# First vectors in eight blocks, turns between two units, attention heads in pairs, a norm's second weights behind its root, and a gate unit three tiles ahead

## The chip, the cores and the metric

The kernel runs on one NeuronCore of a Trainium2 chip. The metric is the time of one execution on the device, in microseconds (us). Five engines work side by side, each through its own instruction list in order, and wait for one another on semaphores: TensorE (PE, matmuls), VectorE (DVE), ScalarE (ACT), GpSimd (POOL) and SyncE (SP). Here POOL and SP only start DMAs. PEld is TensorE's weight load, which overlaps its matmuls. TensorE's clock has two levels, 1.2 and 2.4 GHz, which the profile shows as 0.5 and 1.0.

## The reference

Two layers over 256 latent tokens and 256 context tokens, width 1024, all in float32.

```python
for l in range(DEPTH):                                  # DEPTH = 2
    ml = ada_params(c, mod_w[l], mod_b[l])              # silu(c) @ (1024 x 9216): 9 vectors of 1024
    mc = ada_params(c_ctx, mod_w[l], mod_b[l])
    xl = ffn_half(xl, ml[0:3], ...); xc = ffn_half(xc, mc[0:3], ...)
    hl = modulate(rmsnorm(xl, mix_norm[l]), ml[3], ml[4]); ...
    # even layer: conv group (GLU, depthwise conv 31, LayerNorm, swish) + windowed attention,
    #             8 heads of 64, 2 key heads; odd layer: bidirectional chunked mLSTM
    xl = xl + ml[5] * yl
    xl = ffn_half(xl, ml[6:9], ...); ...
return rmsnorm(xl, final_norm)

def ffn_half(x, mods, g, w_gu, w_d):
    shift, scale, gate = mods
    h = modulate(rmsnorm(x, g), shift, scale) @ w_gu    # 1024 x 5632
    hg, hu = jnp.split(h, 2, axis=-1)
    return x + 0.5 * gate * ((jax.nn.silu(hg) * hu) @ w_d)
```

## The kernel before

Activations lie features on partitions, tokens along the row (512: latent, then context), in 8 tiles of 128 features. Each big product is made of three reduced-precision matmuls (`three`, L429 to L434): high by high, high by low, low by high. The order of every engine is written out by hand.

- **Units.** Weights come in units of 1 MB (`load`, SP). ScalarE copies a unit's high part (`head`, L877), VectorE subtracts to get its low part (`rest`, L1176), TensorE multiplies (`unit`, L444). `raw`, `w_hi`, `w_lo` and two PSUM banks per unit are double: a unit's matmuls start when its low part is made and the unit two before it has been read out (`begin`, L439). A unit is 48 matmuls of 512 columns: 8 tiles, 2 halves, 3 each.
- **Norm n** (0 to 6). ScalarE squares the 8 tiles (L916, L963), VectorE adds them (L1189), TensorE sums over features (L487), ScalarE takes the root (L887), VectorE makes a diagonal of reciprocals (L1214, L1215), TensorE spreads it (L492), and then tile by tile VectorE scales (L1237, `t_ring`), ScalarE rounds to the high part (L895, `hn_hi`), VectorE makes the low part (L1253, `hn_lo`). The first unit behind a norm takes each tile as it comes; the second starts when the first is through.
- **Vectors.** The 18 modulation vectors are 18 jobs. A job is 4 MB of `mod_w` in 4 quarters (`mod_raw`), 16 matmuls for two conditions in each (`mod_products`, L468, four column groups of 32), a copy by ScalarE (`mod_rows`, L910), two small matmuls that turn it (`mod_columns`, L477), and the bias by VectorE (`mod_vector`, L1265). Jobs 0 and 1 stand ahead of the first FFN; others lie behind units, in norms, and jobs 6 to 11 in the attention, a quarter per turn from turn 10 on. A quarter's DMA is started by GpSimd when the quarter before it in its place has been used.
- **Attention** (turns j = 0 to 31, one per head and 128 queries; `s` 0 latent with 512 keys, 1 context with 256). TensorE: `scores` L606, `turn` L615 (transposes), `values` L632. VectorE: `largest` L1402 or L1405, `denominator` L1414, `hn_lo` L1426. ScalarE: `expo` L998, `normalise` L1006, `turned` L1013, `att_head` L1019. Between them VectorE does the depthwise convolution (`taps`, L1359, 124 of 512 elements, 28 of them ahead of turn 0) and TensorE the last two convolution units (`conv_step`), whose sigmoids (L1033) ScalarE does in turns 4 and 9 with a table load before and behind. LayerNorm (L662) follows when all taps are done.
- **od_gate.** Behind norm 4 TensorE does the gate unit (16 columns) and the first key unit tile by tile together (from L703 on), then turns the gate rows (L720); VectorE reads them (L1486), which frees the bank for the next unit.

## Time and profile before

| | us |
|---|---|
| median of 3 runs | 1926.68 (1919.63, 1926.95, 1926.68) |
| profiled execution | 1918.44 |
| its span, first to last instruction | 1916.7 |
| TensorE busy | 1819.4 (95%) |
| VectorE busy | 869.5 (45%) |
| ScalarE busy | 626.4 (33%) |
| mean granted clock of TensorE | 0.974 |

The chain that ended last is TensorE for 90% of the span. The engines' rows give busy time; what matters for this change are the few stretches where TensorE is not full: the start, the norms, the attention and the gate unit.

### The profile page before, as it was taken

The numbers are of one execution on the slowest core, as the hardware profiler recorded it, in microseconds if no ns is written. First come the engines' busy times: TensorE is split into PE (matmuls) and PEld (weight loads), VectorE is DVE, ScalarE is ACT, GpSimd is POOL, SyncE is SP. The second block draws the span as 40 slices with busy tenths as digits, with TensorE's granted clock in tenths as the row PEclk, the third lists the DMA queues.
The fourth block names the chain that finished last, engine by engine and source line by source line (L and its number), as shares of the span: only waits on it lengthen the run. The fifth ranks groups of instructions, "written<-read, shape, count | busy, mean of one in ns | idle before, by whom it ended". The sixth has DMA issues, their size and how long they took to land.

```text
span 1916.7 us, 25184 instructions
## 1 busy us (share of the span) xinstructions
PE 1819.4 (95%) x10083; PEld 1490.1 (78%) x10083; DVE 869.5 (45%) x1335; ACT 626.4 (33%) x849; POOL 36.2 (2%) x72
## 2 busy tenths in 40 slices
PE   3999999999889999999999999999998999899996
PEld 1788888877544668888888688888886998889996
DVE  2433332345878663333233633333344436765554
ACT  2332122223445432222222432222224323544342
POOL 0000000000001000000000000000000000000000
PEclk7999999999899989999999999999998999999998
DMA  8522452243138444222323422233123212354543
GB/s 340 225 88 88 176 191 94 69 153 146 45 130 309 154 158 172 103 83 101 109 71 101 180 88 95 86 105 109 63 93 153 88 67 90 110 197 174 188 170 105
DMA packets 39107, 252.39 MB, mean 132 GB/s; under 512 B 4464, under 2 KB 5872, under 8 KB 14448
## 3 DMA queue, kind: packets, MB, share of 16 engines
q1 hardware_dynamic: 29232, 179.91, 26.5%
q0 software_dynamic: 9792, 71.31, 9.7%
q8 instruction: 61, 1.00, 0.2%
q14 instruction: 22, 0.18, 0.0%
HBM read 250.15 MB, written 1.05 MB: 131 GB/s over the span
## 4 chain that ended last, share of the span: by engine, by line
PE 90%; DVE 5%; ACT 2%; issue 1%; DMA 1%; SPq 0%; ACTq 0%; DVEq 0%
PE ps L432 27%; PE ps L434 27%; PE ps L433 27%; PE ps L468 3%; DVE w_lo L1176 1%; PE ps L632 1%; DMA xT<-in_xT 1%; DVE y L1359 1%; PE ps L606 1%; PE ps L745 1%; PE ps L774 1%; PE ps L492 1%; ACT w_hi L877 1%; PE ps L615 1%; DVE acc L1189 0%
## 5 line engine op out<-in xcount | busy, mean ns | idle before, releaser
L432 PE MATMUL ps<-hn_hi,w_hi 128*128 128x512 f32 (+2 forms) x1784 | 648.6, 364 | 10.2 <-DVE hn_lo L1253 8.3
L433 PE MATMUL ps<-hn_lo,w_hi 128*128 128x512 f32 (+2 forms) x1784 | 640.8, 359 | 0.0
L434 PE MATMUL ps<-hn_hi,w_lo 128*128 128x512 f32 (+2 forms) x1784 | 640.4, 359 | 0.0
L1176 DVE TENSOR_TENSOR w_lo<-raw,w_hi 128x2048 fp32r<-128x2048 f32 (+2 forms) x184 | 377.0, 2049 | 566.3 <-ACT w_hi L877 566.1
L877 ACT ACTIVATE w_hi<-raw 128x2048 fp32r<-128x2048 f32 (+2 forms) x184 | 316.6, 1721 | 777.5 <-PE ps L434 774.1
L432 PEld LDWEIGHTS ps<-hn_hi,w_hi 128*128 128x128 f32 (+1 forms) x1784 | 339.5, 190 | 74.8 <-issue 21.8
L434 PEld LDWEIGHTS ps<-hn_hi,w_lo 128*128 128x128 f32 (+1 forms) x1784 | 339.4, 190 | 50.5
L433 PEld LDWEIGHTS ps<-hn_lo,w_hi 128*128 128x128 f32 (+1 forms) x1784 | 339.8, 190 | 48.6 <-issue 0.5
L432 PE MATMUL ps<-a_hi,w_hi 128*128 128x512 f32 (+1 forms) x704 | 255.6, 363 | 1.7 <-DVE a_lo L1291 1.7
L433 PE MATMUL ps<-a_lo,w_hi 128*128 128x512 f32 (+1 forms) x704 | 255.2, 363 | 0.0
L434 PE MATMUL ps<-a_hi,w_lo 128*128 128x512 f32 (+1 forms) x704 | 255.2, 362 | 0.0
L1194 DVE SCALAR_TENSOR_TENSOR xT<-ps,modT,xT 128x256 f32 (+1 forms) x136 | 59.9, 480 | 226.0 <-PE ps L434 226.0
L432 PEld LDWEIGHTS ps<-a_hi,w_hi 128*128 128x128 f32 x704 | 132.9, 189 | 23.0 <-DVE a_lo L1291 2.1
L434 PEld LDWEIGHTS ps<-a_hi,w_lo 128*128 128x128 f32 x704 | 132.9, 189 | 20.7
L433 PEld LDWEIGHTS ps<-a_lo,w_hi 128*128 128x128 f32 x704 | 132.9, 189 | 20.5
L935 ACT ACTIVATE a_hi<-prod 128x512 f32 (+3 forms) x88 | 50.9, 579 | 212.4 <-DVE prod L1288 212.4
L468 PE MATMUL ps<-mod_raw,c_act 128*32 128x256 f32 x1152 | 81.4, 417 | 17.3 <-DMA mod_raw<-in_mod_w 13.6
L1291 DVE TENSOR_TENSOR a_lo<-prod,a_hi 128x512 f32 (+3 forms) x88 | 55.1, 626 | 71.8 <-ACT a_hi L935 71.8
L1359 DVE SCALAR_TENSOR_TENSOR y<-upad,cols,y 128x512 f32<-128x512 f32 x120 | 82.0, 744 | 0.0
L468 PEld LDWEIGHTS ps<-mod_raw,c_act 128*32 128x32 f32 x1152 | 34.2, 117 | 60.5 <-issue 34.4
L432 PE MATMUL ps<-w_hi,hn_hi 128*128 128x256 f32 x256 | 77.1, 301 | 4.1 <-DVE shared L1486 4.1
L433 PE MATMUL ps<-w_lo,hn_hi 128*128 128x256 f32 x256 | 73.4, 287 | 0.0
(189 smaller groups left out, 1162.4 us busy)
## 6 DMA issues: line engine op xcount, KB each, us to landing
raw<-in_w_up SPq DMA_DIRECT2D x88, 1024.0 KB, 4.8
mod_raw<-in_mod_w POOLq DMA_DIRECT2D x68, 1024.0 KB, 7.3
raw<-in_w_downA SPq DMA_DIRECT2D x32, 768.0 KB, 4.3
raw<-in_w_downB SPq DMA_DIRECT2D x32, 640.0 KB, 3.9
raw<-in_w_od_in SPq DMA_DIRECT2D x16, 1024.0 KB, 4.8
raw<-in_w_ev_in SPq DMA_DIRECT2D x7, 1024.0 KB, 4.8
mod_raw<-in_mod_w SPq DMA_DIRECT2D x4, 1024.0 KB, 10.1
raw<-in_w_ev_out SPq DMA_DIRECT2D x4, 1024.0 KB, 4.8
```

Of the source, the lines that this page charges most:

```text
L432: pe.matmul(o, lh, rh, start=first, stop=False)
L433: pe.matmul(o, lh, rl, start=False, stop=False)
L434: return pe.matmul(o, ll, rh, start=False, stop=last)
L468: last = pe.matmul(ps[32 * g:32 * g + 32, product_bank(m), 0:LAT], c_act[:, k, :], mod_raw[:, k, g * LAT:(g + 1) * LAT], start=(k == 0), s ...
L492: pe.matmul(ps[:, 7, 0:W[n]], ones, rstd[:, 0:W[n]], start=True, stop=True).then_inc(rstd_mm, 1)
L606: pe.matmul(ps[:, 4 + j % 2, k0:KEYS], qk[64 * h2:64 * h2 + 64, tt, a:a + P], qk[64 * h2:64 * h2 + 64, CT, k0:KEYS], start=True, stop=True ...
L877: act.activation(w_hi[:, u0 % 2, 0:n], raw[:, u0 % 2, 0:n], ACT.Copy).then_inc(hi_made, 1)
L935: act.activation(a_hi[:, j + 2 * r, 0:w], prod[:, j, 0:w], ACT.Copy).then_inc(a_hi_made, 1)
L1176: dve.tensor_tensor(w_lo[:, u0 % 2, 0:n], raw[:, u0 % 2, 0:n], w_hi[:, u0 % 2, 0:n], ALU.subtract).then_inc(lo_made, 1)
L1194: last = dve.scalar_tensor_tensor(out=xT[:, d0 + 2 * r, tokens(s)], in0=ps[:, bank(u0, b), tokens(s)], scalar=modT[:, vec, d0 + 2 * r, s:s ...
L1291: dve.tensor_tensor(a_lo[:, j + 2 * r, 0:w], prod[:, j, 0:w], a_hi[:, j + 2 * r, 0:w], ALU.subtract).then_inc(a_made, 1)
L1359: ins = dve.scalar_tensor_tensor(out=dst, in0=src, scalar=col("conv_w", i * CT + c), in1=dst, op0=ALU.mult, op1=ALU.add)
```

## The change

- **First vectors.** Jobs 0 and 1 (shift and scale of norm 0) are laid out anew in 8 blocks of 1 MB: block b holds what tile b of both vectors needs. SP loads `x` first (in 4 parts), then the blocks, two first weight units among them. TensorE does norm 0 ahead of all blocks. The vectors of tile k + 1 are then made while tile k is multiplied: `block_columns(k + 1)` stands behind tile k's matmuls of the first unit, `block_products` behind later ones. GpSimd starts with job 2.
- **Two units in turns.** Behind norms 0, 1, 2, 3 and 5 the first two units share the tiles as they come: 5 tiles in turns (2 for 256 tokens), then the rest of the first unit, then the rest of the second. A job that lay between them still does.
- **Norms.** The first square goes straight into `acc`, the last is added by TensorE (8 small matmuls in place of 4), the clear of `acc` goes. The second unit's high and low part (`LATE_UNIT`) move from ahead of the norm to behind the root.
- **Attention.** 16 turns of a pair of heads in place of 32; `values` alternates the two heads' column groups; context scores share one bank with a wait (`s_half`) and other work between; two quarters of a job per turn; 30 early taps; sigmoids in turns 3 and 9; one pair of banks for the transposes and one for the values in place of two.
- **Gate unit.** It runs alone for three tiles; the keys follow three tiles behind; its rows are turned inside the key unit.

```diff
@@ sync
-            for q in range(4):
-                sp.dma_start(mod_raw[:, 2 * q:2 * q + 2], t["mod_w"][0][:, 2 * q:2 * q + 2]).then_inc(mod_first[q], 16)
-            sp.dma_start(xT[:], t["xT"]).then_inc(x_in, 16)
+            for i in range(4):
+                sp.dma_start(xT[:, 2 * i:2 * i + 2], t["xT"][:, 2 * i:2 * i + 2]).then_inc(x_in[i], 16)
...
+            block(0)
             load(U["f0upA"], 0, 0, t["w_up"][0, 0], UNIT)
+            block(1)
+            load(U["f0upA"], 1, 0, t["w_up"][0, 1], UNIT)
+            for b in range(2, KT):
+                block(b)
@@ tensor
+            def first_units(u0, n, w, between=None):
+                ready = hn_ready(n)
+                order = [(j, k) for k in range(side(w)) for j in range(2)]
+                order += [(j, k) for j in range(2) for k in range(side(w), KT)]
+                for j, k in order:
...
+                    if k == KT - 1:
+                        last.then_inc(unit_mm, 1)
+                        if j == 0 and between:
+                            between()
+                    if n == 0 and j == 0 and k + 1 < KT:
+                        block_columns(k + 1)
+                    if n == 0 and (j, k) in PRODUCTS_BEHIND:
+                        block_products(PRODUCTS_BEHIND[j, k])
...
             def turn(j):
-                if j >= 2:
-                    pe.wait_ge(pT_made, j - 1)
+                if j >= 1:
+                    pe.wait_ge(pT_made, j)
...
+            def values(tt, s):
+                g = 2 * tt + s
+                pe.wait_ge(pT_made, 4 * tt + 2 + s + 1)
+                if g >= 1:
+                    pe.wait_ge(mix_made, g)
...
+                for i, kt in enumerate(att_keys(s)):
+                    for h2 in range(2):
+                        last = pe.matmul(ps[64 * h2:64 * h2 + 64, 0, 0:LAT], v_att[:, kt, 64 * h2:64 * h2 + 64],
+                                         turned_place(s)[:, h2, i, :], start=(i == 0), stop=(kt == 3))
...
+            BEHIND = 3
+            for step in range(KT + BEHIND):
+                if step < KT:
...
+                    last = three(ps[0:16, bank(u), :], weights(u, k * 16, (k + 1) * 16), ...)
+                if step >= BEHIND:
+                    k = step - BEHIND
...
+                    if k < 4:
+                        mod_products(KEY_JOB, k, k + 1)
...
+                    if k == 6:
+                        pe.wait_ge(gate_rows, 1)
@@ scalar
             def norm(n):
                 norm_root(n)
+                head_of(LATE_UNIT[n])
...
+            for k in range(KT):
+                if k == 1:
+                    head_of(1)
+                norm_head(0, k)
+                if k + 1 < KT:
+                    block_rows(k + 1)
@@ vector
             def norm(n):
                 norm_gain(n)
                 norm_rstd(n)
+                rest_of(LATE_UNIT[n])
                 norm_apply(n)
...
+            for k in range(KT):
+                block_vectors(k)
+                norm_scaled(0, k)
+                norm_rest(0, k)
+                if k == 0:
+                    rest_of(1)
```

TensorE ahead of and in the first FFN's first unit, before. `mod_raw` is a job's data, `shared` its row; L432 to L434 are one product in three.

```order
L468 MATMUL ps<-mod_raw,c_act 32x256 [waits mod_in3]
L468 MATMUL ps<-mod_raw,c_act 32x256 x7
L477 MATMUL ps<-sel,shared 128x8 [waits mod_made,mod_row]
L477 MATMUL ps<-sel,shared 128x8
L432 MATMUL ps<-hn_hi,w_hi 128x512 [waits hn_made,lo_made]
L433 MATMUL ps<-hn_lo,w_hi 128x512
L434 MATMUL ps<-hn_hi,w_lo 128x512
L432 MATMUL ps<-hn_hi,w_hi 128x512
```

And after, from the second tile of the first unit on.

```order
L477 MATMUL ps<-hn_hi,w_hi 128x512 [waits hn_made]
L478 MATMUL ps<-hn_lo,w_hi 128x512
L479 MATMUL ps<-hn_hi,w_lo 128x512
L477 MATMUL ps<-hn_hi,w_hi 128x512
L478 MATMUL ps<-hn_lo,w_hi 128x512
L479 MATMUL ps<-hn_hi,w_lo 128x512
L538 MATMUL ps<-sel,shared 128x2 [waits mod_made,mod_row]
L538 MATMUL ps<-sel,shared 128x2
L477 MATMUL ps<-hn_hi,w_hi 128x512
L478 MATMUL ps<-hn_lo,w_hi 128x512
```

The small matmuls that turn the vector of the next tile (`ps<-sel,shared`) stand between the two units' matmuls of a tile, and wait for a row.

VectorE at the end of the first FFN and in the norm behind it, before (`acc` the sum of squares, `w_lo` the low part of weights).

```order
L1194 SCALAR_TENSOR_TENSOR xT<-ps,modT,xT 128x256 [waits unit_mm]
L1194 SCALAR_TENSOR_TENSOR xT<-ps,modT,xT 128x256
L1189 TENSOR_TENSOR acc<-acc,sq 128x512 [waits sq_added,sq_made]
L1176 TENSOR_TENSOR w_lo<-raw,w_hi 128x2048 [waits hi_made]
L1206 SCALAR_TENSOR_TENSOR modT<-modT,cols 128x8 [waits mod_made]
L1206 SCALAR_TENSOR_TENSOR modT<-modT,cols 128x8
L1214 RECIPROCAL inv<-inv 128x4 [waits sd_made,link_v]
L1215 TENSOR_TENSOR rstd<-mats,inv 128x512 [waits link_v]
L1219 MEMSET acc 128x512
L1237 SCALAR_TENSOR_TENSOR t_ring<-xT,modT,ps 128x256 [waits rstd_mm,acc_clear]
```

And after.

```order
L1322 SCALAR_TENSOR_TENSOR xT<-ps,modT,xT 128x256 [waits unit_mm]
L1322 SCALAR_TENSOR_TENSOR xT<-ps,modT,xT 128x256
L1334 SCALAR_TENSOR_TENSOR modT<-modT,cols 128x8 [waits mod_made]
L1334 SCALAR_TENSOR_TENSOR modT<-modT,cols 128x8
L1342 RECIPROCAL inv<-inv 128x4 [waits sd_made,link_v]
L1343 TENSOR_TENSOR rstd<-mats,inv 128x512 [waits link_v]
L1303 TENSOR_TENSOR w_lo<-raw,w_hi 128x2048 [waits hi_made]
L1359 SCALAR_TENSOR_TENSOR t_ring<-xT,modT,ps 128x256 [waits rstd_mm]
L1359 SCALAR_TENSOR_TENSOR t_ring<-xT,modT,ps 128x256 x3
L1366 SCALAR_TENSOR_TENSOR hn_lo<-t_ring,modT,hn_hi 128x256 [waits hn_hi_made]
```

The last sum and the clear are gone, and the second unit's `w_lo` stands behind `rstd` and ahead of the first scaled tile.

TensorE in a turn of the attention that has a quarter of a job, before (`qk` scores, `mats,prod` transposes, `pT,v_att` values).

```order
L468 MATMUL ps<-mod_raw,c_act 32x256 [waits mod_in1]
L468 MATMUL ps<-mod_raw,c_act 32x256 x7
L606 MATMUL ps<-qk 128x256 [waits exp_made]
L615 MATMUL ps<-mats,prod 128x128 [waits pT_made,p_made]
L615 MATMUL ps<-mats,prod 128x128 x3
L632 MATMUL ps<-pT,v_att 64x256 x2
L468 MATMUL ps<-mod_raw,c_act 32x256 [waits mod_in2]
```

And after, the turn with the first quarters.

```order
L702 MATMUL ps<-qk 128x256 [waits exp_made]
L510 MATMUL ps<-mod_raw,c_act 32x256 [waits mod_in0,unit_evac,mod_row]
L510 MATMUL ps<-mod_raw,c_act 32x256 x7
L702 MATMUL ps<-qk 128x256 [waits s_half]
L510 MATMUL ps<-mod_raw,c_act 32x256 [waits mod_in1]
L510 MATMUL ps<-mod_raw,c_act 32x256 x7
L716 MATMUL ps<-mats,sq 128x128 [waits pT_made,p_made]
L716 MATMUL ps<-mats,sq 128x128 x3
L730 MATMUL ps<-pT_ctx,v_att 64x256 [waits mix_made,pT_made]
L730 MATMUL ps<-pT_ctx,v_att 64x256 x3
```

A turn holds both heads' scores around a quarter, a second quarter, four or eight transposes, and both heads' values, which wait for the values before to be read out.

## Rows read from the trace of the kernel before

**Rows 1.** The page: busy time of each engine
```profile
PE 1819.4 (95%) x10083; PEld 1490.1 (78%) x10083; DVE 869.5 (45%) x1335; ACT 626.4 (33%) x849; POOL 36.2 (2%) x72
```

**Rows 2.** Stretches: from:to length, busy (instructions) by engine, clock, DMA share, GB/s
```profile
0.00:47.30 47.30, 15.86 (x146) 8.05 (x146) 12.92 (x25) 12.33 (x19) 4.55 (x12) 0.78 0.84 339
421.40:457.40 36.00, 32.79 (x176) 23.28 (x176) 21.93 (x46) 15.21 (x24) 2.11 (x4) 0.86 0.57 227
500.80:554.80 54.00, 46.82 (x152) 26.44 (x152) 38.99 (x95) 28.95 (x61) 0.00 (x0) 0.85 0.06 20
554.80:636.10 81.30, 75.05 (x586) 33.95 (x585) 66.68 (x164) 41.30 (x121) 12.66 (x24) 0.97 0.89 311
```

**Rows 3.** Order of time, 25 to 47.5: start, length, instruction, idle before
```profile
25.46 1.15 ACT L963 ACTIVATE sq<-xT 128x512 f32<-128x512 f32 x2 [19.31 <-DMA xT<-in_xT]
...
43.34 0.61 PE L477 MATMUL ps<-sel,shared 128*128 128x8 f32 x4 [0.51 <-ACT shared L910]
...
44.48 1.66 DVE L1237 SCALAR_TENSOR_TENSOR t_ring<-xT,modT,ps 128x256 f32<-128x256 f32 x4
...
47.35 0.77 PE L432 MATMUL ps<-hn_hi,w_hi 128*128 128x512 f32 x1 [3.40 <-DVE hn_lo L1253]
```

**Rows 4.** Order of time, TensorE, 50.5 to 76
```profile
51.07 0.40 PE L432 MATMUL ps<-hn_hi,w_hi 128*128 128x512 f32 x1
51.30 0.39 PE L433 MATMUL ps<-hn_lo,w_hi 128*128 128x512 f32 x1
...
60.42 3.66 PE L468 MATMUL ps<-mod_raw,c_act 128*32 128x256 f32 x64
...
75.03 0.51 PE L477 MATMUL ps<-sel,shared 128*128 128x8 f32 x4
```

**Rows 5.** Order of time, the norm behind the first layer's first FFN
```profile
424.76 2.28 DVE L1176 TENSOR_TENSOR w_lo<-raw,w_hi 128x2048 fp32r<-128x2048 f32 x1
...
424.90 1.05 PE L487 MATMUL ps<-mats,acc 128*128 128x1 f32 x8 [1.45 <-DVE acc L1189]
...
425.99 0.26 ACT L887 ACTIVATE inv<-ps,eps 128x4 f32<-128x4 f32 x1 [0.57 <-PE ps L487]
...
428.19 2.08 PE L492 MATMUL ps<-rstd,mats 128*128 128x512 f32 x2 [0.65 <-DVE rstd L1215]
...
430.39 1.65 DVE L1237 SCALAR_TENSOR_TENSOR t_ring<-xT,modT,ps 128x256 f32<-128x256 f32 x4 [1.71 <-PE ps L492]
```

**Rows 6.** Groups, 500.8 to 636.1: shapes, count, busy us, mean ns, idle before
```profile
L1359 DVE SCALAR_TENSOR_TENSOR y<-upad,cols,y 128x512 f32<-128x512 f32 x94 | 64.5, 743 | 0.0
L632 PE MATMUL ps<-pT,v_att 128*64 128x256 f32 x96 | 29.2, 416 | 0.0
...
L606 PE MATMUL ps<-qk 64*128 64x512 f32 x32 | 19.6, 703 | 2.7 <-DVE qk L1379 2.7
...
L1407 DVE TENSOR_SCALAR att_cols<-att_cols 128x1 f32<-128x1 f32 x32 | 6.8, 214 | 1.1
...
L1405 DVE TENSOR_REDUCE att_cols<-ps 128x1 f32<-128x256 f32 x16 | 6.8, 422 | 4.5 <-PE ps L606 4.5
...
L1415 DVE RECIPROCAL att_cols<-att_cols 128x1 f32<-128x1 f32 x32 | 5.3, 164 | 1.1
L1414 DVE TENSOR_TENSOR att_cols<-att_cols 128x1 f32<-128x1 f32 x32 | 4.8, 150 | 0.5 <-ACT att_cols L1000 0.5
...
L1345 DVE TENSOR_TENSOR upad<-t_ring,ps 128x512 f32<-128x512 f32 x2 | 1.4, 690 | 7.4 <-ACT t_ring L1033 7.4
```

**Rows 7.** Order of time, the first matmul behind the gate unit
```profile
1479.33 0.55 PE L432 MATMUL ps<-w_hi,hn_hi 128*128 128x256 f32 x1 [4.07 <-DVE shared L1486]
```

**Rows 8.** Order of time, ScalarE, weights behind the second unit of that norm
```profile
457.45 1.92 ACT L877 ACTIVATE w_hi<-raw 128x2048 fp32r<-128x2048 f32 x1 [7.05 <-PE ps L434]
```

**Rows 9.** Stretches around a stop of TensorE, columns as in 2
```profile
498.10:500.80 2.70, 0.00 (x1) 0.00 (x0) 2.67 (x7) 0.00 (x0) 0.00 (x0) 1.00 0.00 0
501.60:508.00 6.40, 6.40 (x12) 2.81 (x10) 6.26 (x15) 1.42 (x4) 0.00 (x0) 0.50 0.47 165
```

More of the change, by code:

```diff
@@ L417, in _ @@
         def _(pool):
-            for m in range(1, JOBS):
+            for m in range(2, JOBS):
                 if m == JOBS - 1:
@@ L501, in hn_ready, with side @@
                 return ready
+            def side(w):
+                return 5 if w == TOK else 2
+            PRODUCTS_BEHIND = {(1, k): k + 2 for k in range(side(TOK))}
+            PRODUCTS_BEHIND[0, side(TOK)] = side(TOK) + 2
+            def first_units(u0, n, w, between=None):
[3 more added lines that the diff above has]
+                for j, k in order:
+                    if j == 0:
+                        ready(k)
+                    if k == 0:
+                        begin(u0 + j)
+                    for b in range(2):
+                        o = b * KT * P + k * P
+                        last = three(ps[:, bank(u0 + j, b), 0:w], weights(u0 + j, o, o + P),
+                                     (hn_hi[:, k, 0:w], hn_lo[:, k, 0:w]), k == 0, k == KT - 1)
+                    if k == KT - 1:
[6 more added lines that the diff above has]
+                        block_products(PRODUCTS_BEHIND[j, k])
             def ffn(name, f, n, w):
@@ L552, in two @@
                 return b * KT * P + k * P
-            for c in range(2):
-                unit(E + c, 0, 2, KT, TOK, (hn_hi, hn_lo), two, hn_ready(1) if c == 0 else None)
+            pe.wait_ge(mats_in, 16)
+            first_units(E, 1, TOK)
             def rotate(i):
@@ L598, in _, with score @@
             pe.wait_ge(v_made, 1)
-            def scores(j):
-                tt, s, h2, qt = ATT[j]
-                if j >= 2:
+            def score(j, h2):
+                tt, s, qt = ATT[j]
+                if h2 == 0 and j >= 2:
                     pe.wait_ge(exp_made, j - 1)
-                k0 = LAT * s
+                if h2 == 1 and s == 1:
+                    pe.wait_ge(s_half, j // 2 + 1)
                 a = LAT * s + qt * P
-                pe.matmul(ps[:, 4 + j % 2, k0:KEYS], qk[64 * h2:64 * h2 + 64, tt, a:a + P],
-                          qk[64 * h2:64 * h2 + 64, CT, k0:KEYS], start=True, stop=True).then_inc(s_mm, 1)
+                last = pe.matmul(score_place(s)[:, h2, :], qk[64 * h2:64 * h2 + 64, tt, a:a + P],
+                                 qk[64 * h2:64 * h2 + 64, CT, LAT * s:KEYS], start=True, stop=True)
+                if h2 == 1:
+                    last.then_inc(s_mm, 1)
+                elif s == 1:
+                    last.then_inc(s_half, 1)
@@ new lines, in _ @@
+            NJ = len(ATT)
+            pe.wait_ge(unit_evac, E + 5)
+            score(0, 0)
+            score(0, 1)
+            for j in range(NJ + 7):
+                between = [(conv_step, a) for a in CONV_AT.get(j, ())]
+                between += [(mod_products, (m, q, q + 1)) for m, q in att_quarters(j)]
+                if j + 1 < NJ:
+                    score(j + 1, 0)
+                    if ATT[j + 1][1] == 1:
+                        step, a = between.pop(0)
+                        step(*a)
+                    score(j + 1, 1)
+                for step, a in between:
+                    step(*a)
@@ L659, in _ @@
+                for m in att_rows(j):
+                    mod_columns(m)
             pe.wait_ge(pT_made, NJ)
@@ L1224, in norm, with norm_scaled @@
                 norm_rstd(n)
+                rest_of(LATE_UNIT[n])
                 norm_apply(n)
+            def norm_scaled(n, k):
+                if k >= 2 and n < 6:
+                    dve.wait_ge(hn_made, KT * n + k - 1)
+                for s in streams(W[n]):
+                    gain = modT[:, 3 * n + 1, k, s:s + 1] if n < 6 else col(GAIN[n][0], k)
+                    last = dve.scalar_tensor_tensor(out=t_ring[:, k % 2, tokens(s)], in0=xT[:, k, tokens(s)],
+                                                    scalar=gain, in1=ps[:, 7, tokens(s)], op0=ALU.mult, op1=ALU.mult)
+                last.then_inc(t_made if n < 6 else y_made, 1)
@@ L1227, in norm_apply @@
             def norm_apply(n):
-                w = W[n]
-                name = GAIN[n][0]
                 dve.wait_ge(rstd_mm, n + 1)
-                def scaled(k):
-                    if k >= 2 and n < 6:
-                        dve.wait_ge(hn_made, KT * n + k - 1)
-                    for s in streams(w):
-                        gain = modT[:, 3 * n + 1, k, s:s + 1] if n < 6 else col(name, k)
-                        last = dve.scalar_tensor_tensor(out=t_ring[:, k % 2, tokens(s)], in0=xT[:, k, tokens(s)],
-                                                        scalar=gain, in1=ps[:, 7, tokens(s)], op0=ALU.mult, op1=ALU.mult)
-                    last.then_inc(t_made if n < 6 else y_made, 1)
@@ L1311, in down_pair @@
                                 add_square(n + 1, j, r, w)
-                            if end:
+                            if end and (part == "A" or j == 0):
                                 rest_of(down + j + 2 * r + 2)
```

452 lines of the change are left out of this document (243 added, 209 removed).

## The prediction

> **What bounds the kernel now.** I read the page first: TensorE is busy 95% of the span, VectorE 45%, ScalarE 33% [rows 1]. So an edit pays only where TensorE waits, works at half clock, or does less. I then read the stretches that the diff touches by their clock and busy time [rows 2]. At the start TensorE is busy 15.9 of 47.3 us, at a mean clock of 0.78, while DMAs move 339 GB/s. In the first norm and its two units it is busy 32.8 of 36. In the attention it is busy 46.8 of 54.0 and 75.1 of 81.3, VectorE 39.0 and 66.7: neither is full, and they wait for one another by turns. Then the order of time at the start: `x` lands at 25.46, behind a whole job, the columns come at 43.34, the first scaled tile at 44.48, the first product at 47.35 [rows 3]. From there to the end of two units and of job 2 it is TensorE alone, until 75.03 [rows 4]. The norm's rows give its chain from the last sum to the first scaled tile [rows 5], the groups give the attention's VectorE and TensorE work [rows 6], and one row behind the gate unit has a wait of 4.07 [rows 7]. All these together hold less than 50 us of waits. Everything is counted against the profiled execution, 1918.44 (span 1916.7). The runs lie 1.2 to 8.5 above it, their median 8.2; I put the new median 4 above the new sum, the middle of that.
>
> **Start: +0.5 (-5 to +12).** Before, two units (96 matmuls of 512 columns, one per 0.23 us [rows 4]) and job 2 (3.66) run nearly without a stop from 47.35 to 75.03. After, `x` comes first. It lies 4 MB ahead of where it was, 12 us at the measured 339 GB/s [rows 2], so it is there by 13 and norm 0 is over before the first weights are ready: their high part takes 1.9 [rows 8], their low part 2.28 [rows 5], each behind a block and 1 MB of its own (3 us per MB). I put the first unit's first product at 24 and the second unit's, behind its own weight parts, at 30.7. `x`, the 8 blocks and two units are 12 MB, in by 40: DMA doesn't bind.
> From tile 2 on a chain does. The columns of tile k + 1 stand behind tile k's products, since the order puts them there, and tile k + 1 can't start before they are through bias, gain, `t_ring`, the high and the low part: 1.14 from columns to `t_ring` and 2.87 from there to the product, 4.0 in all [rows 3]. With 6 matmuls (1.37) a period is 5.3 to 5.4 us, once per tile, and nobody works ahead. Tiles 2 to 7 then start at 36, 41.3, 46.6, 51.9, 57.2 and 62.5. Up to tile 4 a period also holds 6 matmuls of the second unit and 16 of a later block (0.057 each [rows 4]), so TensorE is busy for 4.3 of 5.3; behind it these are gone and it is idle for 2.4 to 3.3 us per tile. What follows an idle stretch like that is in [rows 9]: TensorE stopped for 2.7 and then ran at 0.50 for 6.4. With half clock from tile 5 on, tile 7 starts near 64, the first unit ends at 66.8, job 2 takes 4.9 (part at half clock) to 71.7, and the second unit's last three tiles (18 matmuls) 4.1 more: 76, with columns 76.7, against 75.6 for the end of those at 75.03. That is +1. At full clock it would be 72.7, or -2.9. I take +0.5, nearer to the first. The upper end is half clock in every period (6.95 instead of 5.35, six times, +10) and some wait for a block.
>
> **Norms 1, 2, 3 and 5: -1 in all (-7 to +3).** The last sum of squares and the wait for `w_lo` of 2.28, which VectorE does while the norm's sum is on TensorE (424.76 and 424.90 [rows 5]), go from ahead of the root's answer; `rstd` comes some 1.5 earlier. But between root and first scaled tile there now stand the same high (1.91) and low part (2.28): root's end 426.25 less 1.5, plus 1.9 behind it, plus 2.3, plus the wait for the spread, is 430.1 against 430.39. So the start stays, within half a microsecond. The gain is behind it. Tiles come each 1.70 us (VectorE's two passes of 0.87), so the first unit alone took 13.6 and the two together 24.1 (433.3 to 457.45, where ScalarE's 1.92 for the next weights waits for the second unit [rows 8]). In turns, 6 matmuls per tile (1.37) fit nearly into that pace: 96 x 0.2275 + 0.6 = 22.5, and if the idle pieces keep half clock for the first tiles, as they do now (clock 0.86 in the stretch [rows 2]), 24.2. Against it: the first unit now ends late, and the third waits until its two banks are read and its weights are made: 1.9 + 2.3 and a gate product 0.7 = 4.9, where the second unit's remaining 18 matmuls cover 4.1. I take -0.5 for norms 1 and 5, 0 for 2 and 3. If the clock rises earlier, it is 1.7 per norm more.
>
> **Gate unit: -2 (-3.7 to 0).** Now gate tile (3 x 0.23 = 0.69) and key tile (12 x 0.119 = 1.43) run together, and behind the rows' turn TensorE waits 4.07, until 1479.33 [rows 7], then runs at half clock for 5 us (some 2.3 lost). The first high tile was at 1452.26, so that is 27.07. After: three gate tiles at the tile pace, 5.1; four steps with a quarter of the key job, 3.2 each, 12.9; one of 2.1; three key tiles 4.3; columns and turn 1.2: 25.7. The 4.07 goes because the rows are turned a tile and a half before the end. But three gate tiles at 0.69 in 1.70 leave TensorE idle a microsecond each, and half clock for some of it is likely: -1.3 from the sum, -2.3 for the old half clock, +1.7 for the new.
>
> **Attention: -14 (-20 to -3).** VectorE: the small passes over 1 element each (6.8, 5.3 and 4.8 us for 32 of each) become 16 of 2: -8.4; eight reductions of 512 in place of 16 of 256, -1; two taps earlier, -1.4 [rows 6]. Of 105.7 busy, 94.8 stay, 92 taps foremost. TensorE: 96 `values` cost 29.2; a pair's go to two column groups of 64 by turns. That column groups run side by side is in the trace: 64 job matmuls of 256 columns, which cycle four groups, take 3.66, 0.057 each [rows 4], the values, in one group, 0.27 at their pace. So values fall to half, -14. Scores (two row groups) I leave as they are.
> Which comes out follows from VectorE's turns, walked with those durations: turns of a pair at 503, 507, 511, 515, then 524.7 (turn 3's sigmoid, whose operand VectorE waits for; two such waits are 7.4 now [rows 6]), 528.6, 532.9, 543, 546.8, 553, then 563.4 (turn 9's sigmoid), 571, 578, 584, 588.5, 594.4, the last taps at 618, and LayerNorm's first matmul behind them at 622, against 636.07. The first job products come later, 561 for 554.8. They need 24 MB, of which four lie ready at the start; twenty at 349 GB/s (311 at a share of 0.89 [rows 2]) take 60 us, so the last is there at 621. The queue is as late as VectorE, which is why the small end of this term is only -3: a second sigmoid wait, a wait of the context scores on their one bank (`s_half`, 8 times 0.5) and that queue.
> What a score pair costs no row shows, since both heads' scores never stood together. A latent pair has four matmuls of 512 columns. One after another they take 4 x 0.61 (19.6 over 32 [rows 6]), 2.4; if two lie side by side, 1.2. I take the first, mostly under VectorE's taps. The Trainium skill, "TensorE: Matmul & The Clock Gate", section "Part 3: Packing small matmuls — row/col tiling", says that a pack spans one matmul plus a few ns per tile. By it the eight latent pairs take 10 us less of TensorE, and with a fifth of that on the path this term would read -16 instead of -14. The column groups' 0.057 agrees with that rule; no row here shows row groups.
>
> **Sum.** +0.5 - 1 - 2 - 14 = -16.5: 1902 for the profiled execution, 1906 as the median.
>
> **Rivals.**
> (a) *The attention gives 3, not 14.* The chain of a turn (scores, maximum, exponent, transposes, values) is longer per pair with one pair of banks in place of two, and 24 MB of quarters start 6 us later. For: VectorE is only 78% busy now, so it waits for this chain. Against: both engines' work falls by 11 and 14. Then 1918.4 - 5.5 + 4 = 1917, no change.
> (b) *Slower: the block chain at half clock.* The place is the first unit. If the clock is down from tile 1 on, every period is 6.95 and the start gives +10 to +12; the third unit's weights wait behind interleaved units, +1 at each of four norms, and the attention gives only 8. It decides when periods pass 6.5 us. Sum +8: 1926 + 4 = 1930, not faster. For: clock 0.50 after 2.7 idle [rows 9]. Against: block products fill the first periods.
> (c) *The gaps that close keep the clock up.* Norms -7, gate -3.7, start -3, attention -14: 1890 + 4 = 1894. For: half clock now follows each gap [rows 2, 9].
>
> **Chances.** Forecast 0.50 (own range 1897 to 1914), (a) 0.17, (b) 0.10, (c) 0.23. The range 1889 to 1924 leaves out most of (b) and the lowest of (c). About 0.5% (9.6 us) can be told from no change. Faster: forecast and (c) less a twentieth, 0.68; same 0.22; slower 0.10.
>
> **What would show it.** First products of tiles 3 to 7 of the first unit 5.3 apart and a clock of 0.5 from tile 5; `t_ring` of norm 1 within 0.5 of 9.0 us behind the last matmul; both units over 22.5 to 24.2 after it; no wait of 4 behind the gate unit; LayerNorm's first matmul 121 us after the first scores, values at half their time. Periods of 7, or attention's first products past 565, would make it wrong on the slow side; tiles made ahead of their turn on the fast side.

## The result, and the profile after

| | before | after |
|---|---|---|
| median (15 runs each) | 1922.42 (1915.29 to 1928.38) | 1917.32 (1913.22 to 1922.38) |
| span of the profiled execution | 1916.7 | 1915.0 |
| TensorE busy | 1819.4 | 1810.1 |

The ratio is 0.9976, interval 0.9965 to 0.9987: 5 us, a quarter of one percent. The interval does not reach 1, so the gain is there, but it is below the 9.6 us that I called telling from no change, and far from the 16.5 of the sum. The page's row of engines, where TensorE and VectorE have lost 9 and 19 us of work [rows 1]:

```profile
PE 1810.1 (95%) x10155; PEld 1495.2 (78%) x10155; DVE 850.9 (44%) x1269; ACT 626.6 (33%) x839; POOL 34.1 (2%) x68
```

The two profiled executions differ by 1.7 us only, where the medians differ by 5.1, so the stretches below come from one execution of each kernel and hold to a microsecond or two each. The difference of the same event in both, after less before, shows where:

| event | before | after | difference | the stretch |
|---|---|---|---|---|
| first job products of norm 1 | 421.52 | 425.02 | +3.5 | start: +3.5 |
| first scores | 500.83 | 503.38 | +2.6 | norm 1: -1.0 |
| LayerNorm's first matmul | 636.07 | 633.22 | -2.9 | attention: -5.4 |
| first job products of norm 3 | 1067.74 | 1065.05 | -2.7 | norm 2 and its FFN: +0.2 |
| first job products of norm 4 | 1440.52 | 1438.43 | -2.1 | norm 3 and its FFN: +0.6 |
| behind the gate's key unit | 1484.49 | 1480.18 | -4.3 | norm 4 and gate: -2.2 |
| first job products of norm 5 | 1697.37 | 1694.88 | -2.5 | od layer's middle: +1.8 |
| end | 1916.7 | 1915.0 | -1.7 | norm 5 and the rest: +0.8 |

**Start.** TensorE in order of time: the first product of each tile of the first unit, with the wait ahead of it in brackets, and job 2. They answer [rows 3, 4].

```profile
25.16 0.80 PE L477 MATMUL ps<-hn_hi,w_hi 128*128 128x512 f32 x1 [1.49 <-DVE hn_lo L1366]
25.75 0.63 PE L478 MATMUL ps<-hn_lo,w_hi 128*128 128x512 f32 x1
26.18 0.63 PE L479 MATMUL ps<-hn_hi,w_lo 128*128 128x512 f32 x1
...
33.36 0.80 PE L477 MATMUL ps<-hn_hi,w_hi 128*128 128x512 f32 x1
...
39.28 0.50 PE L477 MATMUL ps<-hn_hi,w_hi 128*128 128x512 f32 x1 [0.79 <-DVE hn_lo L1366]
...
44.56 0.50 PE L477 MATMUL ps<-hn_hi,w_hi 128*128 128x512 f32 x1 [0.79 <-DVE hn_lo L1366]
...
49.84 0.50 PE L477 MATMUL ps<-hn_hi,w_hi 128*128 128x512 f32 x1 [0.78 <-DVE hn_lo L1366]
...
55.13 0.50 PE L477 MATMUL ps<-hn_hi,w_hi 128*128 128x512 f32 x1 [0.78 <-DVE hn_lo L1366]
...
60.67 0.50 PE L477 MATMUL ps<-hn_hi,w_hi 128*128 128x512 f32 x1 [2.54 <-DVE hn_lo L1366]
...
66.35 0.79 PE L477 MATMUL ps<-hn_hi,w_hi 128*128 128x512 f32 x1 [3.28 <-DVE hn_lo L1366]
...
69.21 5.18 PE L510 MATMUL ps<-mod_raw,c_act 128*32 128x256 f32 x64
```

Tiles 2 to 6 stand 5.28 to 5.54 apart, as the chain was worked out, and every one waits for VectorE's `hn_lo`. Behind tile 5 the waits are 2.54 and 3.28, and job 2 then takes 5.18 for 3.66 [rows 4]: the half clock too is there, if later than forecast, from the end of tile 6 on. But the first two tiles took longer than I had them: 25.16 to 39.28, with a matmul of 512 columns each 0.43 us until 34.8, twice the 0.23 of [rows 4]. (The profile's clock row reads 1.00 in 25 to 34.4; the half speed is read from the durations.) The kernel before began in the same way, just ahead of the first line of [rows 4]:

```profile
47.91 0.63 PE L433 MATMUL ps<-hn_lo,w_hi 128*128 128x512 f32 x1
48.34 0.63 PE L434 MATMUL ps<-hn_hi,w_lo 128*128 128x512 f32 x1
```

**Norm 1**, order of time over all engines, answering [rows 5]:

```profile
429.03 1.90 ACT L986 ACTIVATE w_hi<-raw 128x2048 fp32r<-128x2048 f32 x1
...
430.19 1.57 PE L555 MATMUL ps<-rstd,mats 128*128 128x512 f32 x2 [0.36 <-DVE rstd L1343]
430.96 2.29 DVE L1303 TENSOR_TENSOR w_lo<-raw,w_hi 128x2048 fp32r<-128x2048 f32 x1 [0.83 <-ACT w_hi L986]
...
433.17 1.65 DVE L1359 SCALAR_TENSOR_TENSOR t_ring<-xT,modT,ps 128x256 f32<-128x256 f32 x4
...
436.00 0.47 PE L477 MATMUL ps<-hn_hi,w_hi 128*128 128x512 f32 x1 [2.37 <-issue]
```

The root is early, and the split of `w_hi` and `w_lo` stands where it was put; `t_ring` comes 8.15 behind the first job products, 8.87 before. The two units behind it take 22.5 us from first to last product, for 24.1 before, as the sum had it.

**Attention**, stretches with the columns of [rows 2], the first one norm 1 and its units:

```profile
425.00:459.60 34.60, 30.82 (x183) 22.51 (x183) 20.84 (x44) 16.17 (x25) 2.11 (x4) 0.95 0.51 205
503.40:560.00 56.60, 44.60 (x188) 26.55 (x188) 38.03 (x90) 36.66 (x92) 0.00 (x0) 0.88 0.06 19
560.00:594.00 34.00, 27.32 (x239) 14.68 (x240) 31.59 (x65) 22.73 (x54) 4.22 (x8) 0.85 0.73 283
594.00:633.20 39.20, 28.30 (x310) 13.88 (x309) 24.90 (x47) 8.87 (x22) 8.44 (x16) 0.87 0.99 401
```

Groups from first scores to LayerNorm, answering [rows 6] (busy us, mean ns, idle before and its cause):

```profile
L1497 DVE SCALAR_TENSOR_TENSOR y<-upad,cols,y 128x512 f32<-128x512 f32 x92 | 62.5, 744 | 0.0
L510 PE MATMUL ps<-mod_raw,c_act 128*32 128x256 f32 x384 | 28.5, 426 | 9.6 <-DMA mod_raw<-in_mod_w 9.6
...
L702 PE MATMUL ps<-qk 64*128 64x512 f32 x32 | 10.5, 740 | 3.1 <-DVE qk L1517 2.7 <-ACT att_cols L1127 0.4
...
L730 PE MATMUL ps<-pT_full,v_att 128*64 128x256 f32 x64 | 8.7, 420 | 0.0
...
L730 PE MATMUL ps<-pT_ctx,v_att 128*64 128x256 f32 x32 | 5.2, 454 | 3.2 <-DVE hn_lo L1567 3.2
```

the job products of the same stretch before:

```profile
L468 PE MATMUL ps<-mod_raw,c_act 128*32 128x256 f32 x384 | 27.0, 401 | 3.7 <-ACT shared L910 3.7
```

and the last quarters and LayerNorm's first matmul on TensorE, then VectorE's last taps:

```profile
620.53 1.07 PE L510 MATMUL ps<-mod_raw,c_act 128*32 128x256 f32 x16 [2.44 <-DMA mod_raw<-in_mod_w]
622.96 1.93 PE L510 MATMUL ps<-mod_raw,c_act 128*32 128x256 f32 x16 [1.36 <-DMA mod_raw<-in_mod_w]
...
630.31 1.93 PE L510 MATMUL ps<-mod_raw,c_act 128*32 128x256 f32 x16 [0.21 <-DMA mod_raw<-in_mod_w]
632.75 0.61 PE L518 MATMUL ps<-sel,shared 128*128 128x8 f32 x4 [0.50 <-ACT shared L1021]
633.22 3.68 PE L760 MATMUL ps<-y,mats 128*128 128x512 f32 x8
```

```profile
617.55 4.05 DVE L1497 SCALAR_TENSOR_TENSOR y<-upad,cols,y 128x512 f32<-128x512 f32 x6
```

The reader is to see three things. Values fall from 29.2 to 13.9 us in all, and 32 latent scores from 19.6 to 10.5, more than I took. VectorE's taps are over at 621.6, near the 618 of the walk. And LayerNorm still starts at 633.22, because the products wait for `mod_raw`, 9.6 us in all, in a stretch where the DMA share is 0.99 at 401 GB/s; the last quarter's are at 630.31. Before, no product there waited for a DMA. Over the whole attention TensorE's mean granted clock is 0.87, for 0.92 before, so part of its smaller work is done at half speed: the last quarters' products take 1.93 for 1.07.

**Gate unit**, the turned rows inside the key unit and what follows it; the wait of 4.07 [rows 7] is gone:

```profile
1475.42 0.42 PE L828 MATMUL ps<-mats,gact 16*128 16x16 f32 x4
...
1480.18 0.29 PE L919 MATMUL ps<-shared,mats 128*128 128x16 f32 x2
```

### The profile page after: what moved, and what is told of

Read it like the earlier page. It is cut to its first block, busy times and chain, and to the rows that moved or that the text cites. A ratio compares the mean times of both kernels' runs of the same rounds, so it can differ in the third digit from the quotient of the medians.

```text
span 1915.0 us, 25140 instructions
## 1 busy us (share of the span) xinstructions
PE 1810.1 (95%) x10155; PEld 1495.2 (78%) x10155; DVE 850.9 (44%) x1269; ACT 626.6 (33%) x839; POOL 34.1 (2%) x68
## 4 chain that ended last, share of the span: by engine, by line
PE 86%; DVE 7%; ACT 3%; DMA 2%; issue 1%; SPq 0%; ACTq 0%; DVEq 0%
PE ps L477 27%; PE ps L478 26%; PE ps L479 26%; PE ps L510 2%; DVE y L1497 2%; DVE w_lo L1303 2%; DMA mod_raw<-in_mod_w 1%; ACT w_hi L986 1%; PE ps L854 1%; DVE t_ring L1359 1%; PE ps L883 1%; DVE hn_lo L1366 1%; ACT hn_hi L1002 0%; DVE gact L1541 0%; PE ps L880 0%
## 5 line engine op out<-in xcount | busy, mean ns | idle before, releaser
L1322 DVE SCALAR_TENSOR_TENSOR xT<-ps,modT,xT 128x256 f32<-128x256 f32 (+1 forms) x136 | 59.9, 480 | 228.2 <-PE ps L479 228.2
L477 PEld LDWEIGHTS ps<-a_hi,w_hi 128*128 128x128 f32 x704 | 132.9, 189 | 24.1 <-DVE a_lo L1428 2.1
L510 PE MATMUL ps<-mod_raw,c_act 128*32 128x256 f32 x1024 | 70.9, 413 | 9.6 <-DMA mod_raw<-in_mod_w 9.6
L479 PE MATMUL ps<-w_hi,hn_lo 128*128 128x256 f32 x256 | 72.4, 283 | 0.0
```

Of the source, the lines that this page charges most:

```text
L477: pe.matmul(o, lh, rh, start=first, stop=False)
L479: return pe.matmul(o, ll, rh, start=False, stop=last)
L510: last = pe.matmul(ps[32 * g:32 * g + 32, product_bank(m), 0:LAT], c_act[:, k, :], mod_raw[:, k, g * LAT:(g + 1) * LAT], start=(k == 0), s ...
L1322: last = dve.scalar_tensor_tensor(out=xT[:, d0 + 2 * r, tokens(s)], in0=ps[:, bank(u0, b), tokens(s)], scalar=modT[:, vec, d0 + 2 * r, s:s ...
```

## The experiments

All are edits of the changed kernel, each timed 6 to 12 times; ratios are to the kernel before, timed beside them. Its median moved between 1921.8 and 1923.7, so two experiments are better compared by their ratios than by their medians. In the code `...` stands for lines left out, and long lines are shortened.

**1. Is the start's chain the reason for its loss?**

```diff
-PRODUCTS_BEHIND = {(1, k): k + 2 ...}
+PRODUCTS_BEHIND = {(0, k): k + 2 ...}
 for j, k in order:
+    if n == 0 and j == 0 and k + 1 < KT:
+        block_columns(k + 1)          # ahead of tile k's products
     if j == 0:
         ready(k)
...
-    if n == 0 and j == 0 and k + 1 < KT:
-        block_columns(k + 1)          # was behind them
```

> The changed kernel with the start reordered on TensorE alone: the columns of tile k + 1 stand ahead of tile k's products, and a block's products stand behind the first unit's tile instead of behind the second's. Theory (the start is late because each tile's vectors are made only when the tile before has been multiplied, a chain of 5.28 us per tile): the distance between first products of tiles falls from 5.28 to about 4.3 where TensorE has a block and two units' tiles to do, and to about 3.6 behind that; tile 7 of the first unit starts near 57 instead of 66.35, and all behind it is 9 to 12 us earlier, so about 1906 us against 1917. Rival (the start is bound by the blocks' DMA or by the half clock at its beginning): the distances stay near 5.3 or a wait on a block's DMA appears, and the total moves by less than 3 us.

Measured: 1905.4 us, ratio 0.9906 (0.9882 to 0.9930). First products of tiles 2 to 7 of the first unit there (tile 2 at 36.28, tile 4 is left out):

```profile
36.28 0.47 PE L477 MATMUL ps<-hn_hi,w_hi 128*128 128x512 f32 x1
...
40.70 0.47 PE L477 MATMUL ps<-hn_hi,w_hi 128*128 128x512 f32 x1
...
49.56 0.47 PE L477 MATMUL ps<-hn_hi,w_hi 128*128 128x512 f32 x1
...
53.21 0.50 PE L477 MATMUL ps<-hn_hi,w_hi 128*128 128x512 f32 x1
...
56.58 0.50 PE L477 MATMUL ps<-hn_hi,w_hi 128*128 128x512 f32 x1 [1.72 <-DVE hn_lo L1366]
```

4.42 apart as long as TensorE has 4.3 of work per tile, then 3.65 and 3.37. Norm 1's job products start at 412.48, 12.5 earlier than after the change and 9.0 earlier than before it. Of the 12.5, 3.0 are there by tile 2, 6.8 come between tiles 2 and 7, and 2.8 behind it, where tile 7 and job 2 (3.66) now run at full clock. The order of a few small matmuls, and of the block's products beside them, was worth the whole loss and more; no run moves one of the two alone. Nothing later gave it back: LayerNorm's first matmul is 11.1 earlier too.

**2. Do transfers set the attention's end?** The quarters of jobs 6 to 11 are loaded by half (those vectors are then not computed from all weights).

```diff
-pool.dma_start(mod_raw[:, 2 * q:2 * q + 2], t["mod_w"][m - 2][:, 2 * q:2 * q + 2])
+pool.dma_start(mod_raw[:, 2 * q:2 * q + (1 if m in ATT_JOBS else 2)],
+               t["mod_w"][m - 2][:, 2 * q:2 * q + (1 if m in ATT_JOBS else 2)])
```

> The changed kernel, where the 24 quarters of jobs 6 to 11 (those used in the attention) are loaded by half only, 0.5 MB each; the products run over what else lies there, so those vectors are not computed from all their weights. All instructions and their order stay. Theory (the attention's end is set by the transfers: 24 MB at the full rate of 401 GB/s, the walked turns end with VectorE's taps near 618): TensorE's waits for these quarters, 9.6 us, go, and LayerNorm's first matmul comes at 619 to 624 instead of 633.2; the total is 9 to 14 us shorter than the changed kernel's, some 1905. Rival (the chain of turns with one pair of banks sets the end): LayerNorm's first matmul stays within 3 us of 633.

Measured: 1905.12, ratio 0.9916 (0.9899 to 0.9932), 12 us below the changed kernel. The same stretches, then LayerNorm:

```profile
560.00:594.00 34.00, 27.47 (x222) 14.45 (x222) 31.28 (x64) 22.44 (x53) 4.22 (x8) 0.80 0.56 181
594.00:620.00 26.00, 23.46 (x307) 13.00 (x306) 25.12 (x48) 9.19 (x23) 7.39 (x14) 1.00 0.79 262
```

```profile
622.21 3.68 PE L761 MATMUL ps<-y,mats 128*128 128x512 f32 x8
```

Rates fall to 181 and 262 GB/s, and from first scores to LayerNorm it is 119.5 us (502.74 to 622.21) instead of 129.8. Forecast had been 121. TensorE's waits for these quarters fall from 9.6 us to 2.4. The chain of turns, then, was forecast rightly and the transfers were not; the rival that the single pair of banks holds the end at 633 falls.

**3. Quarters earlier in the attention.**

```diff
-at = [2 * (j - ATT_FROM) + i for i in range(2)]
+at = {0: range(4), 1: range(4, 8)}.get(j - ATT_FROM,
+      range(2 * (j - ATT_FROM) + 4, 2 * (j - ATT_FROM) + 6))
...                                   # nothing ahead of turn 10; rows follow one turn behind
```

> The changed kernel, with the attention's job quarters dealt out anew: four in turn 10 and four in turn 11, then two per turn, in place of two per turn from turn 10 on; rows and columns of each job follow one turn behind its last quarter. Theory (the attention's end is set by 20 MB of quarters whose transfers start only when the first quarters are used): DMA share in 565 to 594 rises from 0.8 to over 0.95, no product waits longer in all, and LayerNorm's first matmul comes 5 to 9 us earlier than 633.2. Rival (the chain of turns or VectorE's taps set the end): it moves by less than 2 us, with the quarters' waits gone.

Measured: 1915.63, ratio 0.9959 (0.9942 to 0.9976), an interval that overlaps the change's own. First scores to LayerNorm took 128.3, LayerNorm's first matmul stayed (633.60), the waits for quarters grew from 9.6 to 12.7 us, and the DMA share in 560 to 594 did not rise (0.68; the first product is at 568.17 there). Both theory and rival missed: the theory had the matmul 5 to 9 us earlier, the rival had the waits gone. What the theory left out: in turn 11 TensorE waits for the quarters (3.59 us), and scores and transposes stand behind it in order.

**4. One job out of the attention**, so that 20 MB of quarters stay of 24.

```diff
-DOWN_JOB = {"f0A": 3};  NORM_JOB = {1: 5, ...};  ATT_JOBS = range(6, 12)
+DOWN_JOB = {"f0A": 3, "f0B": 5};  NORM_JOB = {1: 6, ...};  ATT_JOBS = range(7, 12)
```

> The changed kernel with one job (4 MB, 64 products) taken out of the attention: job 5 goes behind the first down unit of the first FFN's second part, job 6 into norm 1, and the attention has jobs 7 to 11. Theory (transfers set the attention's end): the attention is 8 to 11 us shorter from first scores to LayerNorm's first matmul (129.8 now), the job costs 4 to 4.5 us of TensorE where it goes, so 4 to 7 us shorter in all. Rival (they don't): the attention stays, and the total is 4 us longer.

Measured: 1909.49, ratio 0.9940 (0.9919 to 0.9961). The attention took 118.0 (508.08 to 626.04), 11.8 less, and norm 1 came 3.4 later. The theory's way, and more of it: 8 to 11 were expected for the attention, 4 to 7 in all, where the medians give 7.8. The rival falls.

**5. Both, and then all three.**

> The two edits that the theory says are worth something, together: columns ahead of the tiles (11.9 us shorter by itself) and one job moved out of the attention. If the stretches are independent, the sum: 4 to 7 us below the first alone, 1899 to 1902. Rival (the clock falls elsewhere for what is closed here, or the attention is bound otherwise): no less than 1904.

Measured: 1899.81, ratio 0.9890 (0.9873 to 0.9908), the fastest kernel here, 22 us below the kernel before. The edits nearly add: 11.9 and 7.8 by themselves, 17.5 together.

> Columns ahead, one job moved out of the attention, and the quarters dealt out four and four at first. With 20 quarters in place of 24 the transfers end within 2 to 3 us of VectorE's taps, so the earlier start should give little more. Theory: attention from first scores to LayerNorm's first matmul 117 to 120 (120.3 without the last edit), total 1897 to 1901. Rival (transfers still set it): 115 or less and 1896 or less.

Measured: 1910.73, ratio 0.9935 (0.9922 to 0.9948): 9 us worse by the ratios (11 by the medians) than without the early quarters. Both theory and rival missed. TensorE at turn 11 and at LayerNorm:

```profile
579.54 1.94 PE L512 MATMUL ps<-mod_raw,c_act 128*32 128x256 f32 x16 [3.88 <-DMA mod_raw<-in_mod_w]
...
622.32 1.96 PE L762 MATMUL ps<-y,mats 128*128 128x512 f32 x4
627.78 2.74 PE L762 MATMUL ps<-y,mats 128*128 128x512 f32 x4 [3.50 <-DVE y L1499]
```

The first product of the fourth quarter in turn 11 waits 3.88 us, VectorE's turns behind it are pushed back (its last taps end at 628.4, for 617.4 without the edit), and now it is the taps that LayerNorm waits for, 3.50 us in its middle. From first scores to the end of LayerNorm's sums it is 134.0 us (496.55 to 630.52), against 125.4 (497.16 to 622.57) without the edit: 8.6, and the spans differ by 8.2. In these two kernels, then, a transfer that is waited for in the middle of a turn costs every engine, and a wait at the end costs only TensorE. TensorE's granted clock in 555 to 590 is 0.74 there, for 0.85 without the edit; how much of the 8.6 is the wait and how much the half clock around it, no run separates.

**6. The weights' split behind the root.**

```diff
 def norm(n):                        # ScalarE; VectorE alike
-    norm_root(n)
     head_of(LATE_UNIT[n])
+    norm_root(n)
```

> The changed kernel, with the second unit's high and low part put back ahead of the norm's root and reciprocals, in norms 1 to 5; the last sum on TensorE, the turns and all else stay. Theory (the split behind the root costs what it gives): the first scaled tile of norm 2 stands within 0.7 us of where it does now, counted from the end of the last residual, and the total within 2 us of the changed kernel's. Rival (the split behind the root is a gain): first scaled tiles 1.5 us or more later per norm and the total 5 us or more longer. Second rival (it is a loss, since high and low part of 4.2 us now stand between root and first tile): 1 us or more earlier per norm, the total 3 us or more shorter.

Measured: 1915.73, ratio 0.9961 (0.9947 to 0.9975): the total does not tell it from the change. In norm 1:

```profile
429.11 2.29 DVE L1303 TENSOR_TENSOR w_lo<-raw,w_hi 128x2048 fp32r<-128x2048 f32 x1 [2.50 <-ACT w_hi L986]
...
432.55 0.50 PEld L555 LDWEIGHTS ps<-rstd,mats 128*128 128x128 f32 x2 [2.59 <-DVE rstd L1343]
...
434.66 1.65 DVE L1359 SCALAR_TENSOR_TENSOR t_ring<-xT,modT,ps 128x256 f32<-128x256 f32 x4 [2.17 <-PE ps L555]
...
437.49 0.77 PE L477 MATMUL ps<-hn_hi,w_hi 128*128 128x512 f32 x1 [1.00 <-issue]
```

Seen from the first job products, the first high tile comes at 11.86, 13.11, 11.82 and 11.91 in norms 1 to 4, against 10.98, 12.27, 10.92 and 11.03 after the change: the split behind the root gives 0.9 at each. (In norm 2, from the last residual to the first scaled tile it is 0.84, just over the theory's 0.7 and far from either rival.) It does not reach the total. In the trace two stretches take it back: from the first high tile behind norm 4 to behind the key unit it is 29.1 us here and 30.7 after the change, and the od layer's middle is 212.9 for 214.7. TensorE's wait ahead of the tiles is one piece of 2.4 to 3.7 us after the change and two shorter ones here, so half clock is a likely reason; but the 29.1 comes in other runs too (experiments 4 and 9) and the 212.9 in experiment 8, and the cause is open.

**7. The units in turns.**

```diff
-order = [(j, k) for k in range(side(w)) for j in range(2)]
+turns = side(w) if n == 0 else 0
+order = [(j, k) for k in range(turns) for j in range(2)]
```

> The changed kernel, with the first two units behind norms 1, 2, 3 and 5 one after the other again (tile by tile the first, then the second), and norm 0's start as it is. Theory (the turns fill TensorE at the tiles' pace of 1.70 but make the third unit wait for its banks and weights): first to last product of the two units 24.1 instead of 23 or so behind norm 1, no wait ahead of the third unit; the total 0 to 3 us longer than the changed kernel's. Rival (the turns give 1.5 us or more in each of four norms): 6 us or more longer.

Measured: 1914.78, ratio 0.9956 (0.9941 to 0.9971), not slower. From the first high tile to the next mark: norm 1 to first scores 67.65 (67.38 in turns), norm 2 to norm 3's job 366.5 (366.6), norm 3 to norm 4's job 361.4 (362.5). First to last product of the two units is 24.15 there and 22.5 in turns, and no wait stands ahead of the third unit there, as expected. The turns are worth nothing all the same: what they fill, the third unit waits for, here behind norm 1 after the change:

```profile
459.62 0.47 PE L477 MATMUL ps<-hn_hi,w_hi 128*128 128x512 f32 x1 [1.07 <-DVE upad L1483]
```

**8. The gate unit as before**, with the rows turned behind the loop:

```diff
-BEHIND = 3
+BEHIND = 0
...
-if k == 6:
-    (four transposes of the gate's rows)
 last.then_inc(unit_mm, 1)
+(four transposes of the gate's rows)
```

> The changed kernel with the gate unit and the first key unit tile by tile together again, and the gate rows turned behind them; all else stays. Theory: TensorE waits some 4 us for the rows' read behind the transposes and runs at half clock after it; first high tile to the first matmul behind is 27 us instead of 25 or so, the total 1.5 to 4 us longer. Rival (the wait only moves, half clock is then paid elsewhere): within 1 us.

Measured: 1920.95, ratio 0.9996 (0.9985 to 1.0007), so the edit is worth 0.2%, 3.6 us of medians.

```profile
1480.25 0.43 PE L477 MATMUL ps<-w_hi,hn_hi 128*128 128x256 f32 x1 [3.47 <-DVE shared L1622]
...
1484.69 0.29 PE L918 MATMUL ps<-shared,mats 128*128 128x16 f32 x2
```

The wait of 3.47 is back, and from first high tile (1450.76) to behind the key unit it is 33.9 us; 30.7 after the change (1449.46 to 1480.18), 32.2 before it. The theory holds for the wait and the total. Its levels did not: to the first matmul behind the unit it had 27 for 25, and it is 29.5 for 27.8.

**9. The values' column groups.**

```diff
-for i, kt in enumerate(att_keys(s)):
-    for h2 in range(2):
+for h2 in range(2):
+    for i, kt in enumerate(att_keys(s)):
```

> The changed kernel with the attention's values one head after the other again instead of the two heads' column groups by turns. Theory of the matmul: 96 values take 25 to 29 us instead of 14, as before the change. Theory of the end: the transfers still set it, so LayerNorm's first matmul and the total stay within 2.5 us (the later half of the turns has slack). Rival (TensorE sets it): LayerNorm's first matmul and the total 8 us or more later.

Measured: 1920.51, ratio 0.9979 (0.9970 to 0.9988), the change's own ratio.

```profile
L730 PE MATMUL ps<-pT_full,v_att 128*64 128x256 f32 x64 | 13.0, 414 | 0.0
...
L730 PE MATMUL ps<-pT_ctx,v_att 128*64 128x256 f32 x32 | 5.2, 454 | 2.5 <-DVE hn_lo L1567 2.4
```

Values took 18.2 us, not 25 to 29. So only 4.3 of the 15.3 that the change saved come from the turns of column groups; the other 11 us of busy time are left for what both orders share, the values of a head in one run instead of in halves. That is by subtraction; no run has the halves by themselves. The eight context groups cost 5.2 either way. The profiled execution, the slowest of the 11, has 134.5 from scores to LayerNorm, 4.7 more, outside the theory's 2.5 and short of the rival's 8. The median doesn't show it: the end's theory stands by the total alone.

## Why the prediction was wrong

**Attention (-14 forecast, -5.4 measured): the step that failed.** It is the queue of quarters. The sum took LayerNorm at 622, "behind" VectorE's last taps, and set the queue beside it with "the last is there at 621". VectorE's walk was right: its sixteen turns came 0.8 to 2.6 us behind the walked times, in an attention that itself began 2.6 later, and its work fell to 94.5 us, forecast 94.8. Counted from the first scores (500.8 in the sum, 503.38 measured), the queue was mis-sized in three places:

- Its start. The first job products stand 62.0 behind the first scores, for 60.2: +1.8.
- Its length. From the first quarter's products to the last one's it is 65.0 us (565.35 to 630.31), for 60: +5.0. I counted twenty quarters, 21.0 MB, at 349 GB/s. In these 65.0 us the DMAs moved 24.2 MB at 372 GB/s: 2.1 MB of weights for the next units and 1.0 of the next job's quarters share them. And they were not full all the time. Each quarter's transfer waits for the use of the quarter before it in its place, and the second pair is used only 12.6 us behind the first (577.97), so the share is 0.86 up to 594 and 0.99 behind it.
- Its end. LayerNorm stands 2.9 behind the last quarter's first product, for 1: the products (1.93, half speed), the copy of the row and the columns still follow.

That is 8.7, and 8.6 is what the term was off. The queue was put into the small end of the term; it belonged in its middle. The sign named for this, first products past 565, did come (565.35). With half the bytes the stretch is 119.5 (experiment 2), and with 20 quarters it is 118.0 (experiment 4), so nothing else held it at 129.8. TensorE's part of the sum was right in size for another reason than mine: of the 15.3 us that the values lost, the column groups' turns are 4.3 (experiment 9). That my -14 for them was nearly met is luck.

**Start (+0.5 forecast, +3.5 measured).** The mechanism and the period were right (5.3), and a half clock came as forecast, though from the end of tile 6 on and not from tile 5. The tiles' start was not: 39.28 for tile 2, forecast 36. The first product came 1.2 late (25.16 for 24), and I gave the first two tiles the full clock's durations; TensorE did them at 0.43 per 512 columns, half speed, and block 2's products took 1.94 for 1.07. The lines of [rows 4] begin at 51.07, just behind the stretch in which the kernel before shows the same. That I chose a value between the two clocks, "nearer to the first", cost another half microsecond. Rival (b) had this at +10 and did not come: from tile 2 on the periods were those of full clock.

**Norms (-1 forecast; -0.2 measured in the stretches of 1, 2 and 3, and +0.8 in that of 5, which runs to the end).** "So the start stays, within half a microsecond" was a little off: in norm 1 the first scaled tile came 0.7 earlier. The turns' 1.6 was there (24.1 to 22.5 us), but the wait that I named against them, the third unit's banks, took it back (experiment 7). I should have let it cancel the whole gain, as it did.

**Gate unit (-2 forecast, -2.2 measured with norm 4)**, right in size, 0.7 of it ahead of the first high tile and 1.5 behind. To the first matmul behind the unit it was 27.8 us, forecast 25.7, but the half clock that followed there before, 2.3 us, is gone. Experiment 8 puts the edit at 3.2 in the trace. With the gate unit alike, the stretch is 33.9 against 32.2 before, so 1.7 went elsewhere; I put it down to half clock behind the longer wait in norm 4 (3.73 for 1.52 us): four gate tiles and a quarter of the job run at half speed there (0.63 for 0.39 us), none before. No run tests it by itself, and the stretch is not the same each time: 30.7 in six of the kernels with the new gate unit, 31.2 in one, and 29.1 in experiments 4, 6 and 9, two of them with the same wait of 3.7.

**Not forecast: +1.8 in the od layer's middle**, which the change does not touch. The trace has clock 0.96 after and 1.00 before in 40 us of it (from 80 us behind the key unit on), and 0.93 after for 0.96 before in the last 50. At those lengths it is some 3 us more of half clock in each, 1.6 us lost in the first alone (an estimate from these means). It is no accident of one execution: the stretch takes 214.4 to 214.9 us in nine of the eleven kernels with the change, and 212.9 and 212.7 in experiments 6 and 8, which did not have the first of the two; 212.9 before. Why the clock falls there is open.

Of the rivals, (a) is the one that came: it had the attention nearest (-3) and named both causes, the turns' chain and the quarters' late start; only the transfers were at work. That it also met the 1917 is in part luck, since it has no loss of 3.5 at the start and none of 1.8 in the od layer, and since the median stood 0.1 above the profiled execution where I had put 4. I gave it 0.17, though the queue's end stood in my own walk a microsecond from VectorE's. Terms that end in a tie of two estimates each several us wide should be priced by the later of both with its own spread, not by the nearer one.

## What to carry to other kernels

When an edit makes the engines faster, ask what queue they then reach: write the bytes that must pass behind the first use, all users of the DMAs counted, divide by the rate of a full stretch, and add what still follows the last byte. A small dependent step that feeds the next tile belongs ahead of this tile's work, not behind it; that move, with the products beside it, was worth more than twice the whole change. And a wait for a transfer on an in-order engine should stand where nobody else's work is queued behind it.
